# Turning the residual at five seams by DMA instead of TensorE, with two chunks by tiles of tokens, in a two-layer mixer trunk

## The chip, the cores and the metric

One core of one Trainium2 chip runs the kernel. The metric is the device time of one execution in microseconds; lower is better. Engines are called as in the profile: PE is TensorE, DVE is VectorE, ACT is ScalarE, POOL is GpSimd, SP is SyncE, which here only issues DMAs.

## What is computed

256 tokens (two tiles of 128) of width 1024 pass two layers, in float32. Each layer is

```
x = x + 1/2 * SwiGLU_1(RMSNorm(x))                    # 1024 -> 2 x 2816 -> 1024
u = RMSNorm(x);  [q|k|v|g|p|c|gates] = u @ W_in       # mixer input, blocks of 512 columns
x = x + (sig(g_ret)*y_ret + sig(g_pool)*y_pool + sig(g_conv)*y_conv) @ W_out
x = x + 1/2 * SwiGLU_2(RMSNorm(x))
```

and a last RMSNorm follows. The three branches are a chunkwise retention with rotary, a multi-scale mean pooling, and a gated causal convolution of 31 taps with a LayerNorm. Between two of these stages stands what is called a seam here: x is complete for the one, and needed turned (features on partitions) by the next. There are five seams besides the kernel's start: in layer 0 after the first FFN, before the second FFN, then between the layers, and the first two again in layer 1.

## The kernel before

**Products.** Every big product is made in three matmuls: the weights and the turned activations are each split in a high part of type fp32r and the rest (`w_hi`, `w_lo`, `xT_hi`, `xT_lo`), and `product` adds high by high, high by low and low by high in PSUM. The activations are the operand that is loaded (128x128), the weights the one that moves (512 columns). `in_block(l, g, t)` makes chunk g (1024 x 512) for tile of tokens t: 8 products of three, 24 matmuls. `wide` makes 1024 output columns from some 128-row tiles, as two halves n = 0, 1 of 512 columns. The order is written out by hand, in a function for each engine; there is no scheduler.

**Weights.** They come in halves of chunks, 1 MB each, through a ring of seven slots (`raw`, in which `w_lo` is made in place), all from SyncE's queue, in order of use. ScalarE casts a half to `w_hi` (`cast(hf)`, ring of five), VectorE makes `w_lo` (`sub(hf)`). A load waits until the half seven before it is used, a cast until the half five before it is used (`wait_half_used`); a half is used once both tiles of tokens have passed it.

**Hidden activations.** In an FFN, the product of silu and gate is turned by the DMA: ScalarE splits the four bytes of each value into two planes of 16 bits (`split_h`, tile `h_planes`), SyncE issues a DMA transpose of the planes (`turn_h`, tile `hT_planes`), VectorE joins them (`h_merge`, tile `hT_whole`). SyncE issues it in its stream of loads, behind a load with a given number.

**The seam.** VectorE adds the product to x, one quarter (tile of tokens t, 512 columns c) at a time (`add_next`). `turn_x` has TensorE transpose the quarter in four matmuls with the identity into PSUM (`tr`, two banks). ScalarE makes `xT_hi` with the norm's gain (`x_high`, 4 instructions), VectorE `xT_lo` (`x_low`, 4 instructions). The quarters of tokens 0 are turned amid the last chunk's products of tokens 1, those of tokens 1 amid the next stage's first block of tokens 0. `finish` and `begin` are the other engines' parts of this. The norm's scale comes later (`rs`), on the block's result, from `square` on ScalarE and GpSimd's `norm_factor`.

**The mixer's VectorE.** It also computes the 124 convolution taps, which are placed by hand in groups, `conv_taps(l, n)`, between other work; `decayed` scales the retention's scores into `st`, for which `inner` on TensorE waits.

**The end.** For each tile of tokens: add to x, square and sum on ScalarE, power on GpSimd, scale by ScalarE and VectorE, store.

Of the kernel before, what the change touches and what calls it, by code (L numbers as in the profile page):

```python
# [15 lines left out]
P = 128  # L16
L = 2
# [55 lines left out]
def out_bank(n):  # L73
    return 1 - n
# [23 lines left out]

ADDS_BEFORE = {0: CHUNKS - 1, 1: MIX - 1, 3: FFN2 - 1}


def trunk(nc, x_in, positions, weights_in, gate_bias, pool_scale, norm_final, params, ident_in,
          inv_freq_in, decay_in, band_in, out):
    with ExitStack() as ctx:
# [29 lines left out]
        end_small = sb("end_small", [P, 5, T])  # L134
        end_meansq = end_small[:, 0:2, :]
        end_eps, end_total, end_rs = (end_small[:, i, :] for i in range(2, 5))
# [35 lines left out]
        hT_whole = place("hT_whole", [P, 2, S])  # L172
        ffn_end, end[0] = end[0], arena_at
# [56 lines left out]
        x_hi_ready = sem("x_hi_ready")  # L230
        hT_hi_ready = sem("hT_hi_ready")
# [45 lines left out]
        end_weighted = sem("end_weighted")  # L277
        out_ready = [sem(f"out_ready{n}") for n in (0, 1)]
# [10 lines left out]
        def gain(l, norm, k):  # L289

            if l == 0 and norm == 0:
                return ident_gain[:, P + k:P + k + 1]
            return par[:, l, PAR_GAIN[norm] + k:PAR_GAIN[norm] + k + 1]

# [39 lines left out]
        def _(pe):  # L334
# [28 lines left out]
            def in_block(l, g, t, norm=None, mid={}):  # L363
# [4 lines left out]
                for k in range(KT):  # L368
# [7 lines left out]
                    if norm is not None and k % 4 == 0:  # L376
                        wait_tr_taken(pe, ("x", l, norm, t, k // 4))
# [8 lines left out]

            def wide(l, g, use, t, lhs, ks, first, last, mid={}):
# [3 lines left out]
                for n in (0, 1):  # L391
                    b = out_bank(n)
                    if first:
                        wait_acc_free(l, use, t, n, b)
                    for i, k in enumerate(ks):
                        hf = l * HALVES + 2 * g + i // m
                        if t == 0 and n == 0 and i % m == 0:
# [3 lines left out]
                                     first and i == 0, last and i == len(ks) - 1)  # L401
# [13 lines left out]
            def turn_x(l, norm, t, c):  # L415
                if l == 0 and norm == 0:
                    pe.wait_ge(x_landed[t][c], 16)
                elif norm == 0:
                    wait_acc_taken(pe, l - 1, FFN2 + FB, t, c)
                else:  # L420
                    wait_acc_taken(pe, l, FB if norm == 1 else M_OUT, t, c)
                transpose4(("x", l, norm, t, c),
# [23 lines left out]
            def ffn(l, f, after):  # L446

                g0, norm = f * FFN2, 3 * f
                in_block(l, g0, 0, norm, {3: lambda: turn_x(l, norm, 1, 0),
                                          5: lambda: turn_x(l, norm, 1, 1)} if l + f == 0 else  # L450
                         {1: lambda: turn_x(l, norm, 1, 0), 4: lambda: turn_x(l, norm, 1, 1)})
                in_block(l, g0, 1, norm)
                for b in range(1, FB):
# [1220 lines left out]
```

## Time and profile before

| | |
|---|---|
| time, median of 3 runs | 1152.99 us (1152.76 to 1153.17) |
| the profiled execution's own time | 1152.98 us |
| its span in the trace | 1151.1 us |
| TensorE busy | 1140.0 us |
| VectorE busy | 780.0 us |
| ScalarE busy | 608.7 us |
| granted clock of TensorE | 0.999 of full |
| DMA | 234.70 MB, mean 204 GB/s |

The span runs from the first to the last instruction that the profiler saw; the time has a little around it. Busy times are sums over the whole span. A matmul's record is longer than the distance to the next one, since they are pipelined: what it costs is that distance. In a group's row, the numbers behind the first bar are busy us and mean ns of one, behind the second the idle time ahead of it and what ended it.

### The profile page before, as it was taken

The numbers are of one execution on the slowest core, as the hardware profiler recorded it, in microseconds if no ns is written. First come the engines' busy times: TensorE is split into PE (matmuls) and PEld (weight loads), VectorE is DVE, ScalarE is ACT, GpSimd is POOL, SyncE is SP. The second block draws the span as 40 slices with busy tenths as digits, with TensorE's granted clock in tenths as the row PEclk, the third lists the DMA queues.
The fourth block names the chain that finished last, engine by engine and source line by source line (L and its number), as shares of the span: only waits on it lengthen the run. The fifth ranks groups of instructions, "written<-read, shape, count | busy, mean of one in ns | idle before, by whom it ended". The sixth has DMA issues, their size and how long they took to land.

```text
span 1151.1 us, 13215 instructions
## 1 busy us (share of the span) xinstructions
PE 1140.0 (99%) x5150; PEld 939.9 (82%) x5150; DVE 780.0 (68%) x953; ACT 608.7 (53%) x703; POOL 41.9 (4%) x67
## 2 busy tenths in 40 slices
PE   8999999999999999999999999999999999999997
PEld 6888888888878888888888888888888788888886
DVE  6656465699997766655465656367999976565543
ACT  7655445453655565555365554364637356555442
POOL 2000000000100010000010000020001001000000
PEclk9999999999999999999999999999999999999999
DMA  9966564563754566756576757455638645676640
GB/s 368 323 196 218 182 235 170 218 177 134 247 211 170 196 204 208 239 167 231 185 260 194 231 188 233 173 212 174 201 119 262 231 146 191 221 242 205 174 183 37
DMA packets 92942, 234.70 MB, mean 204 GB/s; under 512 B 62912, under 2 KB 63296, under 8 KB 68048
## 3 DMA queue, kind: packets, MB, share of 16 engines
q1 hardware_dynamic: 90384, 226.78, 58.6%
q0 software_dynamic: 1648, 6.06, 1.7%
q10 hardware_dynamic: 848, 1.02, 0.3%
q8 instruction: 41, 0.67, 0.2%
q14 instruction: 21, 0.17, 0.0%
HBM read 218.11 MB, written 1.05 MB: 190 GB/s over the span
## 4 chain that ended last, share of the span: by engine, by line
PE 86%; DVE 10%; ACT 2%; issue 1%; DMA 0%; POOLq 0%; ACTq 0%; DVEq 0%; POOL 0%
PE acc L352 28%; PE acc L354 28%; PE acc L353 28%; DVE y L1236 4%; DVE w_lo L1036 3%; PE tr L412 2%; ACT w_hi L675 1%; ACT pin L822 0%; DVE gates L1311 0%; DVE gates L1256 0%; DVE ua L1292 0%; DVE qk L1301 0%; DMA ident_gain<-in_ident 0%; PE tr L482 0%; DVE sideT_lo L1354 0%
## 5 line engine op out<-in xcount | busy, mean ns | idle before, releaser
L675 ACT CAST w_hi<-raw 128x2048 fp32r<-128x2048 f32 (+1 forms) x206 | 379.1, 1851 | 260.4 <-PE acc L354 255.9
L1036 DVE TENSOR_TENSOR w_lo<-raw,w_hi 128x2048 fp32r<-128x2048 f32 (+1 forms) x206 | 448.4, 2211 | 95.0 <-ACT w_hi L675 94.9
L352 PE MATMUL acc<-w_hi,xT_hi 128*128 128x512 f32 x1184 | 466.3, 394 | 1.0 <-DVE w_lo L1046 0.6
L354 PE MATMUL acc<-w_hi,xT_lo 128*128 128x512 f32 x1184 | 461.3, 390 | 0.0
L353 PE MATMUL acc<-w_lo,xT_hi 128*128 128x512 f32 x1184 | 460.9, 389 | 0.0
L352 PEld LDWEIGHTS acc<-w_hi,xT_hi 128*128 128x128 f32 x1184 | 222.4, 188 | 47.1 <-DVE gates L1311 1.5
L354 PEld LDWEIGHTS acc<-w_hi,xT_lo 128*128 128x128 f32 x1184 | 222.2, 188 | 47.0
L353 PEld LDWEIGHTS acc<-w_lo,xT_hi 128*128 128x128 f32 x1184 | 222.5, 188 | 44.4
L1099 DVE SCALAR_TENSOR_TENSOR h<-acc,rs,silu_gate 128x256 f32<-128x256 f32 x88 | 42.5, 483 | 175.2 <-ACT silu_gate L731 175.2
L352 PE MATMUL acc<-w_hi,hT_hi 128*128 128x512 f32 x352 | 137.5, 391 | 0.0
L354 PE MATMUL acc<-w_hi,hT_lo 128*128 128x512 f32 x352 | 137.0, 389 | 0.0
L353 PE MATMUL acc<-w_lo,hT_hi 128*128 128x512 f32 x352 | 136.9, 389 | 0.0
L731 ACT ACTIVATE silu_gate<-acc,rs 128x256 f32<-128x256 f32 x88 | 41.9, 476 | 121.7 <-PE acc L354 120.8
L1236 DVE SCALAR_TENSOR_TENSOR y<-uT,par,y 128x256 f32<-128x256 f32 x240 | 97.1, 476 | 0.0
L354 PEld LDWEIGHTS acc<-w_hi,hT_lo 128*128 128x128 f32 x352 | 66.1, 188 | 13.7
L353 PEld LDWEIGHTS acc<-w_lo,hT_hi 128*128 128x128 f32 x352 | 66.1, 188 | 13.5
L352 PEld LDWEIGHTS acc<-w_hi,hT_hi 128*128 128x128 f32 x352 | 66.1, 188 | 13.5
L716 ACT COPY h_planes<-h 128x512 uint16<-128x512 uint16 x88 | 50.1, 620 | 4.8 <-DMA hT_planes<-h_planes 4.8
L692 ACT ACTIVATE xT_hi<-tr,par 128x128 fp32r<-128x128 f32 x80 | 22.9, 369 | 36.6 <-PE tr L412 36.6
L1084 DVE COPY hT_whole<-hT_planes 128x1024 uint16<-128x1024 uint16 x44 | 33.3, 757 | 10.4 <-DMA hT_planes<-h_planes 10.3
L1053 DVE SCALAR_TENSOR_TENSOR x<-acc,x 128x512 f32<-128x512 f32 x24 | 16.5, 689 | 28.7 <-PE acc L354 28.7
L1072 DVE SCALAR_TENSOR_TENSOR xT_lo<-tr,par,xT_hi 128x128 fp32r<-128x128 f32 x80 | 22.5, 343 | 15.5 <-ACT xT_hi L692 15.0
(122 smaller groups left out, 568.2 us busy)
## 6 DMA issues: line engine op xcount, KB each, us to landing
raw<-in_weights SPq DMA_DIRECT2D x194, 1024.0 KB, 4.8
raw<-in_weights SPq DMA_DIRECT2D x10, 512.0 KB, 3.6
bias<-in_gate_bias POOLq DMA_DIRECT2D x6, 512.0 KB, 7.8
raw<-in_weights SPq DMA_DIRECT2D x8, 256.0 KB, 4.8
scale_row<-in_pool_scale POOLq DMA_DIRECT2D x2, 512.0 KB, 8.7
x<-in_x SPq DMA_DIRECT2D x3, 256.0 KB, 8.0
band<-in_band POOLq DMA_DIRECT2D x1, 768.0 KB, 6.2
hT_planes<-h_planes SPq DMA_TRANSPOSE x44, 3.1
```

The source lines that it names most:

```text
L352: nc.tensor.matmul(o, a_hi, b_hi, start=first, stop=False)
L353: nc.tensor.matmul(o, a_hi, b_lo, start=False, stop=False)
L354: return nc.tensor.matmul(o, a_lo, b_hi, start=False, stop=last)
L412: mm = nc.tensor.transpose(bank(name)[:, i * P:(i + 1) * P], s, ident)
L675: nc.scalar.copy(w_hi[:, hf % HIGHS, 0:n], raw[:, hf % RAWS, 0:n]).then_inc(hi_split, 1)
L692: nc.scalar.activation(xT_hi[:, k, tokens(t)], bank(("x", l, norm, t, c))[:, i * P:(i + 1) * P], ACT.Copy, scale=gain(l, norm, k)).then_in ...
L716: nc.scalar.copy(h_planes[:, :, :, t, :], h[:, t, :].bitcast(U16).rearrange("p (k n a) -> p a k n", k=2, a=2)).then_inc(h_split, 1)
L731: nc.scalar.activation(silu_gate[:, t, :], acc[:, t, IN_BANK[g], 0:256], ACT.Silu, scale=rs[:, t:t + 1]).then_inc(silu_ready, 1)
L1036: nc.vector.tensor_tensor(w_lo[:, hf % RAWS, 0:n], raw[:, hf % RAWS, 0:n], w_hi[:, hf % HIGHS, 0:n].bitcast(F32), ALU.subtract).then_inc(l ...
L1084: nc.vector.tensor_copy(hT_whole[:].rearrange("p k n -> p (k n)").bitcast(U16) .rearrange("p (m a) -> p a m", a=2), hT_planes[:]).then_inc ...
L1099: nc.vector.scalar_tensor_tensor(h[:, t, :], acc[:, t, IN_BANK[g], 256:512], rs[:, t:t + 1], silu_gate[:, t, :], ALU.mult, ALU.mult).then_ ...
L1236: a = nc.vector.scalar_tensor_tensor(y[:, c, :], u, par[:, l, w:w + 1], y[:, c, :], ALU.mult, ALU.add)
```

## The change

1. At the five seams (`SEAM`) x is turned as the hidden activations are. Each quarter is split into planes by ScalarE (`split_x`), turned by a DMA transpose from SyncE (`turn_x`), joined by VectorE (`x_join`) into `x_whole`; `x_high` and `x_low` then read that and not PSUM. The planes are those of the hidden activations, one set. TensorE transposes x only at the kernel's start.
2. TensorE's order. An FFN's last two output chunks, and the two of `W_out`, are run for tokens 0 both, and then for tokens 1 both. The next stage's first two chunks are run in the same way (`two_blocks`): both for tokens 0, then both for tokens 1.
3. The order on ScalarE and VectorE around the seams follows (`seam`), and the first blocks' silu, hidden and take steps after it.
4. Some `conv_taps` and one `sub` in the mixer are moved; the wait of the conv product is made in two steps.
5. At the end, the last chunk's product for tokens 1, columns 512 to 1023, is made in two pieces of 256 columns in a bank of its own (`last_products`), each added, squared and weighted by itself; the chunks before it are closed and added earlier.

```diff
+SEAM = {key: i for i, key in enumerate([(0, 1), (0, 3), (1, 0), (1, 1), (1, 3)])}
...
+        x_planes = h_planes[:].rearrange("p a k t n -> p a (k t) n")
+        xT_planes = hT_planes
+        x_whole = hT_whole[:].rearrange("p k n -> p (k n)").rearrange("p (k n) -> p k n", n=P)
...
                     if norm is not None and k % 4 == 0:
-                        wait_tr_taken(pe, ("x", l, norm, t, k // 4))
+                        if (l, norm) in SEAM:
+                            pe.wait_ge(x_lo_ready, piece(l, norm, t, k // 4) + 1)
+                        else:
+                            wait_tr_taken(pe, ("x", l, norm, t, k // 4))
...
+            def two_blocks(l, g, norm, mid={}):
+
+                in_block(l, g, 0, norm)
+                in_block(l, g + 1, 0)
+                in_block(l, g, 1, norm, mid)
+                in_block(l, g + 1, 1)
...
+                    closed = last or (l, g, t, n) == (L - 1, CHUNKS - 2, 1, 1)
...
+                if after:
+                    for t in range(T):
+                        step(final - 1, t)
+                        step(final, t)
+                else:
+                    for i in (final - 1, final):
+                        step(i, 0)
+                        step(i, 1)
...
+            def last_products(l, g, ks):
+
+
+                m = len(ks) // 2
+                for i, k in enumerate(ks):
+                    hf = l * HALVES + 2 * g + i // m
+                    mm = product(acc[:, 1, out_bank(0), :], hT(k, 1), weights(hf, i % m * D, NB),
+                                 False, i == len(ks) - 1)
+                done(mm, (l, g, 1, 0))
+                for part in (0, 1):
+                    for i, k in enumerate(ks):
+                        hf = l * HALVES + 2 * g + i // m
+                        mm = product(ret[:, part, 0:256], hT(k, 1),
+                                     weights(hf, i % m * D + NB + part * 256, 256),
+                                     i == 0, i == len(ks) - 1)
+                    done(mm, (l, g, 1, 1 + part))
...
-                in_block(l, M_A, 0, 1, {1: lambda: turn_x(l, 1, 1, 0),
-                                        4: lambda: turn_x(l, 1, 1, 1)})
-                in_block(l, M_A, 1, 1)
-                in_block(l, M_B, 0)
-                in_block(l, M_B, 1, mid={3: lambda: turn_u(l, 0)})
+                two_blocks(l, M_A, 1, {5: lambda: turn_u(l, 0)})
...
-                pe.wait_ge(conv_lo_ready, l * 2 + 2)
-                wide(l, M_CONV, M_CONV, 0, side, range(4), True, True)
+                pe.wait_ge(conv_lo_ready, l * 2 + 1)
+                wide(l, M_CONV, M_CONV, 0, side, range(4), True, True,
+                     {(0, 1): lambda: pe.wait_ge(conv_lo_ready, l * 2 + 2)})
...
+                wait_tr_taken(pe, ("m", l, 0, 1))
+                wide(l, M_OUT + 1, M_OUT, 0, xT, range(4, 8), False, True)
                 wait_tr_taken(pe, ("m", l, 1, 0))
                 wide(l, M_OUT, M_OUT, 1, xT, range(4), True, False)
-                wait_tr_taken(pe, ("m", l, 0, 1))
-                wide(l, M_OUT + 1, M_OUT, 0, xT, range(4, 8), False, True)
                 wait_tr_taken(pe, ("m", l, 1, 1))
-                wide(l, M_OUT + 1, M_OUT, 1, xT, range(4, 8), False, True,
-                     {(0, 0): lambda: turn_x(l, 3, 0, 0), (0, 2): lambda: turn_x(l, 3, 0, 1)})
+                wide(l, M_OUT + 1, M_OUT, 1, xT, range(4, 8), False, True)
...
+            def turn_x(l, norm, t, c):
+                at = piece(l, norm, t, c)
+                sp.wait_ge(x_split, at + 1)
+                sp.wait_ge(x_joined, at)
+                sp.dma_start_transpose(xT_planes[:].rearrange("p a (g n) -> p (a g) n", n=P),
+                                       x_planes.rearrange("p a k n -> p (a k n)")
+                                       ).then_inc(x_turned, 16)
...
+                for at, norm in ((0, 0), (MIX, 1), (FFN2, 3)):
+                    if (hf // HALVES, norm) in SEAM:
+                        for ahead, t, c in ((2, 0, 0), (2, 0, 1), (5, 1, 0), (6, 1, 1)):
+                            if hf % HALVES == 2 * at + ahead:
+                                turn_x(hf // HALVES, norm, t, c)
...
+            def split_x(l, norm, t, c):
+
+                wait_x(l, norm, t, c)
+                act.wait_ge(x_turned, 16 * piece(l, norm, t, c))
+                nc.scalar.copy(x_planes,
+                               x[:, t, columns(c)].bitcast(U16)
+                               .rearrange("p (k n a) -> p a k n", k=4, a=2)).then_inc(x_split, 1)
...
+            def seam(l, norm, hf):
+
+                split_x(l, norm, 0, 0)
+                square(l, norm, 0)
+                split_x(l, norm, 0, 1)
+                x_high(l, norm, 0, 0)
+                cast(hf + 1)
+                cast(hf + 2)
+                x_high(l, norm, 0, 1)
+                split_x(l, norm, 1, 0)
+                cast(hf + 3)
+                split_x(l, norm, 1, 1)
                 x_high(l, norm, 1, 0)
+                cast(hf + 4)
+                square(l, norm, 1)
                 x_high(l, norm, 1, 1)
...
+            def x_join(l, norm, t, c):
+
+                dve.wait_ge(x_turned, 16 * (piece(l, norm, t, c) + 1))
+                dve.wait_ge(x_lo_ready, piece(l, norm, t, c))
+                nc.vector.tensor_copy(hT_whole[:].rearrange("p k n -> p (k n)").bitcast(U16)
+                                      .rearrange("p (m a) -> p a m", a=2), xT_planes[:]
+                                      ).then_inc(x_joined, 1)
...
+            def seam(l, norm, hf):
+
                 add_next(l, norm, 0, 0)
                 add_next(l, norm, 0, 1)
+                x_join(l, norm, 0, 0)
                 x_low(l, norm, 0, 0)
+                x_join(l, norm, 0, 1)
+                sub(hf + 1)
                 add_next(l, norm, 1, 0)
                 x_low(l, norm, 0, 1)
+                add_next(l, norm, 1, 1)
+                sub(hf + 2)
+                x_join(l, norm, 1, 0)
+                sub(hf + 3)
+                x_low(l, norm, 1, 0)
+                x_join(l, norm, 1, 1)
+                sub(hf + 4)
+                x_low(l, norm, 1, 1)
...
-                conv_taps(l, 18)
+                conv_taps(l, 14)
...
-                conv_taps(l, 8)
+                conv_taps(l, 12)
...
+            add_last(acc[:, 1, out_bank(1), :], columns(1), (L - 1, CHUNKS - 2, 1, 0))
...
+            for part in (0, 1):
+                s = slice(NB + part * 256, NB + part * 256 + 256)
+                dve.wait_ge(end_added, part + 1)
+                add_last(ret[:, part, 0:256], s, (L - 1, CHUNKS - 1, 1, 1 + part))
+                dve.wait_ge(end_added, part + 2)
+                weigh(1, s)
+            dve.wait_ge(end_weighted, 5)
+            scale_out(1)
```

How this moves instructions, at the first seam (end of layer 0's first FFN, start of the mixer). In `order`'s rows a name is the tile's. **VectorE, before**, from the adds of tokens 0 (x2) to the subtractions after the seam; the rows of `w_lo` are `sub`, those of `xT_lo` are `x_low`:

```order
L1053 SCALAR_TENSOR_TENSOR x<-acc,x 128x512 x2
L1072 SCALAR_TENSOR_TENSOR xT_lo<-tr,par,xT_hi 128x128 x4
L1053 SCALAR_TENSOR_TENSOR x<-acc,x 128x512
L1072 SCALAR_TENSOR_TENSOR xT_lo<-tr,par,xT_hi 128x128 x4
L1053 SCALAR_TENSOR_TENSOR x<-acc,x 128x512
L1036 TENSOR_TENSOR w_lo<-raw,w_hi 128x2048
L1072 SCALAR_TENSOR_TENSOR xT_lo<-tr,par,xT_hi 128x128 x8
L1366 MEMSET uT 128x4x30
L1036 TENSOR_TENSOR w_lo<-raw,w_hi 128x2048 x2
```

**VectorE, now**, from the same two adds; `hT_whole<-hT_planes` is `x_join`:

```order
L1170 SCALAR_TENSOR_TENSOR x<-acc,x 128x512 x2
L1187 COPY hT_whole<-hT_planes 128x2x512
L1198 SCALAR_TENSOR_TENSOR xT_lo<-hT_whole,par,xT_hi 128x128 x4
L1187 COPY hT_whole<-hT_planes 128x2x512
L1153 TENSOR_TENSOR w_lo<-raw,w_hi 128x2048
L1170 SCALAR_TENSOR_TENSOR x<-acc,x 128x512
L1198 SCALAR_TENSOR_TENSOR xT_lo<-hT_whole,par,xT_hi 128x128 x4
L1170 SCALAR_TENSOR_TENSOR x<-acc,x 128x512
L1153 TENSOR_TENSOR w_lo<-raw,w_hi 128x2048
L1187 COPY hT_whole<-hT_planes 128x2x512
L1153 TENSOR_TENSOR w_lo<-raw,w_hi 128x2048
L1198 SCALAR_TENSOR_TENSOR xT_lo<-hT_whole,par,xT_hi 128x128 x4
```

Three of the four joins are in these rows; the fourth follows, with the `sub` of A+4 and the last `x_low`. A is the mixer's first half of weights. The three `sub` shown are those of A+1 (the first block's second half), A+2 and A+3 (the second block's second half); the last stands right behind the third join, where before the last two `x_low` (the x8) stood ahead of the `sub` of A+3 (in the x2).

**SyncE, before**, the loads between the FFN's last turns of `h` and the mixer's first turns of q and k:

```order
L636 DMA raw<-in_weights 128x2048 x2
L601 DMA_TRANSPOSE hT_planes<-h_planes 128x8x128
L636 DMA raw<-in_weights 128x2048 x19
L610 DMA_TRANSPOSE qkT_planes<-qk_planes 128x8x128 x2
L636 DMA raw<-in_weights 128x2048 x2
L610 DMA_TRANSPOSE qkT_planes<-qk_planes 128x8x128 x2
```

**SyncE, now**, from the last turn of `h`; L661 is `turn_x`:

```order
L653 DMA_TRANSPOSE hT_planes<-h_planes 128x8x128
L696 DMA raw<-in_weights 128x2048 x8
L661 DMA_TRANSPOSE hT_planes<-h_planes 128x8x128 x2
L696 DMA raw<-in_weights 128x2048 x3
L661 DMA_TRANSPOSE hT_planes<-h_planes 128x8x128
L696 DMA raw<-in_weights 128x2048
L661 DMA_TRANSPOSE hT_planes<-h_planes 128x8x128
L696 DMA raw<-in_weights 128x2048 x7
L670 DMA_TRANSPOSE qkT_planes<-qk_planes 128x8x128 x2
```

Of the four turns of x, the first two are issued behind the load of A+2, the third behind that of A+5 and the fourth behind that of A+6. The one behind A+5 is thus issued when three loads have gone out since the second turn: A+3, A+4 and A+5.

## Rows read from the trace of the kernel before

**Rows 1.** The page, busy time by engine:
```profile
PE 1140.0 (99%) x5150; PEld 939.9 (82%) x5150; DVE 780.0 (68%) x953; ACT 608.7 (53%) x703; POOL 41.9 (4%) x67
```

**Rows 2.** TensorE timeline, 100 to 104 us: start, length, operation; first and last:
```profile
99.65 0.39 PE L352 MATMUL acc<-w_hi,xT_hi 128*128 128x512 f32 x1
...
103.96 0.39 PE L353 MATMUL acc<-w_lo,xT_hi 128*128 128x512 f32 x1
```

**Rows 3.** Groups by line, TensorE:
```profile
L412 PE MATMUL tr<-ident_gain,x 128*128 128x128 f32 x96 | 14.9, 279 | 1.0 <-DMA x<-in_x 0.6 <-DMA ident_gain<-in_ident 0.4
```

**Rows 4.** Waits of TensorE: us in total, times, longest us:
```profile
PE ret L501 <- DVE st L1284: 1.3, 2, 0.6
...
PE acc L352 <- DVE sideT_lo L1354: 0.4, 2, 0.2
```

**Rows 5.** Timeline at the first seam, TensorE around a four of transposes:
```profile
185.10 0.39 PE L354 MATMUL acc<-w_hi,hT_lo 128*128 128x512 f32 x1
...
186.93 0.39 PE L354 MATMUL acc<-w_hi,hT_lo 128*128 128x512 f32 x1
```

**Rows 6.** Timeline of VectorE in the first mixer, ahead of `decayed`:
```profile
266.19 7.21 DVE L1236 SCALAR_TENSOR_TENSOR y<-uT,par,y 128x256 f32<-128x256 f32 x18
```

**Rows 7.** Timeline of TensorE in the pool product, first and ninth row:
```profile
299.96 0.28 PE L352 MATMUL acc<-w_hi,sideT_hi 128*128 128x256 f32 x1
...
300.92 0.28 PE L354 MATMUL acc<-w_hi,sideT_lo 128*128 128x256 f32 x1
```

**Rows 8.** Groups by line and shape, operations like those of the last stage:
```profile
L1099 DVE SCALAR_TENSOR_TENSOR h<-acc,rs,silu_gate 128x256 f32<-128x256 f32 x88 | 42.5, 483 | 175.2 <-ACT silu_gate L731 175.2
L1053 DVE SCALAR_TENSOR_TENSOR x<-acc,x 128x512 f32<-128x512 f32 x24 | 16.5, 689 | 28.7 <-PE acc L354 28.7
...
L1013 ACT ACTIVATE squares<-x 128x512 bf16<-128x512 f32 x4 | 2.5, 631 | 18.0 <-DVE x L1053 18.0
```

**Rows 9.** Groups by line and shape, ScalarE, then VectorE:
```profile
L675 ACT CAST w_hi<-raw 128x2048 fp32r<-128x2048 f32 x194 | 368.3, 1910 | 249.0 <-PE acc L354 244.5 <-DMA raw<-in_weights 4.5
...
L802 ACT COPY qk_planes<-qk 128x1024 uint16<-128x1024 uint16 x8 | 8.3, 1036 | 0.0
...
L1036 DVE TENSOR_TENSOR w_lo<-raw,w_hi 128x2048 fp32r<-128x2048 f32 x194 | 436.8, 2283 | 95.0 <-ACT w_hi L675 94.9
...
L1084 DVE COPY hT_whole<-hT_planes 128x1024 uint16<-128x1024 uint16 x44 | 33.3, 757 | 10.4 <-DMA hT_planes<-h_planes 10.3
...
L1072 DVE SCALAR_TENSOR_TENSOR xT_lo<-tr,par,xT_hi 128x128 fp32r<-128x128 f32 x80 | 22.5, 343 | 15.5 <-ACT xT_hi L692 15.0
```

**Rows 10.** Instructions on tile hT_planes, SyncE: the 44 turns, and their landings:
```profile
L601 SPq DMA_TRANSPOSE hT_planes<-h_planes x44: 1232/1232/1392, 29.8 to 1088.8; - x44
...
DMA to landing us min/median/max: 3.0/3.1/9.7
```

**Rows 11.** The page, DMA issues: KB each, median us from issue to landing:
```profile
raw<-in_weights SPq DMA_DIRECT2D x194, 1024.0 KB, 4.8
```

**Rows 12.** Tile raw, the second load of a pair: at 384.6, at 191.2:
```profile
DMA to landing us min/median/max: 6.6/6.6/6.6
...
DMA to landing us min/median/max: 7.8/7.8/7.8
```

**Rows 13.** Tile raw, the five loads from 5.1 to 7.4 us:
```profile
L636 SPq DMA_DIRECT2D raw<-in_weights x5: 453/473/693, 5.1 to 7.4; - x5
...
DMA to landing us min/median/max: 10.2/14.0/17.8
```

**Rows 14.** A load at 233.9, then a turn of qk_planes at 234.7:
```profile
L636 SPq DMA_DIRECT2D raw<-in_weights x1: 327/327/327, 233.9 to 233.9; - x1
...
DMA to landing us min/median/max: 5.6/5.6/5.6
...
L610 SPq DMA_TRANSPOSE qkT_planes<-qk_planes x1: 1231/1231/1231, 234.7 to 234.7; - x1
...
DMA to landing us min/median/max: 5.7/5.7/5.7
```

More of the change, by code:

```diff
@@ L770, in ffn @@
+                for b in range(2, FB):
+                    silu(l, f, b - 1, 1)
+                    cast(ahead(b))
+                    split_h(l, f, b - 1, 0)
+                    split_h(l, f, b - 1, 1)
+                    silu(l, f, b, 0)
+                    h_high(l, f, b - 2)
+                    cast(ahead(b) + 1)
+                final = len(OUT_CHUNKS) - 1
+                for i in range(final):
+                    hf = ahead(FB + i)
                     if i == 0:
@@ L988, in mixer @@
                 merged_high(l, 1, 1)
-                cast(ahead(M_OUT) + 1)
-                finish(l, 3, ahead(M_OUT + 1))
+                seam(l, 3, ahead(M_OUT))
             act.wait_ge(ident_landed, 16)
@@ L1022, in _ @@
                               weighted[:, t, columns(0)]).then_inc(stored, 16)
+            for n in (0, 1):
+                wait_acc_taken(act, L - 1, FFN2 + FB, 0, n)
+                last_square(0, columns(n), n)
+            store(0)
+            wait_acc_taken(act, L - 1, FFN2 + FB, 1, 0)
+            last_square(1, columns(0), 0)
+            for part in (0, 1):
+                act.wait_ge(end_added, part + 2)
+                last_square(1, slice(NB + part * 256, NB + part * 256 + 256), 1 + part)
+            store(1)
         @block.vector
@@ new lines, in ffn @@
+                if l + f == 0:
+                    x_low(0, 0, 1, 0)
+                    x_low(0, 0, 1, 1)
+                    for hf in (2, 3, 4):
+                        sub(hf)
+                    hidden(l, f, 0, 0)
+                    hidden(l, f, 0, 1)
+                    sub(ahead(1) - 1)
+                    sub(ahead(1))
+                    hidden(l, f, 1, 0)
+                else:
+                    hidden(l, f, 0, 0)
+                    hidden(l, f, 1, 0)
+                    sub(ahead(1) - 1)
+                    hidden(l, f, 0, 1)
+                    sub(ahead(1))
@@ L1151, in ffn @@
                         dve.wait_ge(par_landed, 16)
-                    finish(*after, l * HALVES + 2 * (g0 + FFN_CHUNKS - 1) + 3)
+                    seam(*after, ahead(FFN_CHUNKS - 2))
             setup = [0]
```

259 lines of the change are left out of this document (140 added, 119 removed).

## The prediction, made before the run

> **What bounds the kernel now.** I read the page first, then TensorE's groups, its waits, its timeline in a quiet stretch and at a seam, then the other engines' groups by shape, and last the landings of single transfers. The page is there to name the engine: TensorE is busy for 1140.0 of 1151.1 us [rows 1]. The quiet stretch gives its beat: from the first to the last row shown, 19 matmuls lie 4.31 us apart, 0.227 us each, though one lasts 0.39 us [rows 2]. So time can only come out of matmuls that need not be there, out of waits, and out of the two ends. The groups show such matmuls: 96 transposes of x in 24 fours [rows 3]. The waits show nearly nothing else: 1.3 us at the retention's inner products (twice 0.6) and 0.4 us at the conv side (twice 0.2); none is at a seam [rows 4]. Whatever replaces the transposes must therefore arrive in time, as they do now.
>
> **What goes.** The seam's timeline prices a four: the matmul before it starts at 185.10, and the sixth product matmul after that one at 186.93 [rows 5]. Six beats are 1.36 us, so the four costs 0.47 us. Five seams have four such groups each; the first four groups of the kernel stay. Twenty by 0.47 is 9.4 us off the path.
>
> The two waits named above are served by other edits. Four conv taps are moved from ahead of `decayed` to behind it; 18 taps take 7.21 us, so four take 1.6 us, more than the 0.6 us for which TensorE waits on `st` [rows 6, 4]. The conv side's wait is split so that the first half's products start on the first half. I take both away whole: 1.7 us.
>
> At the end, the last 512 columns are made as two pieces of 256. A 256-column matmul has a beat of 0.12 us (0.96 us for eight) [rows 7], so 24 of them take 2.88 us where twelve whole ones took 2.72: +0.16. Behind the last one, a DVE operation of 256 columns takes 0.48 against 0.69 us, and the square 0.63 us for 512 columns, of which I save 0.2 (between nothing and half) [rows 8]. Net about -0.3 us, and between +0.2 and -0.5. What follows (the power, the scaling, the store) is as long as before.
>
> So 9.4 + 1.7 + 0.3 = 11.4 us are to be had if nothing new is late.
>
> **What is added.** Each of the 20 pieces of x (512 columns of 128 tokens) now takes a split by ScalarE, like the row of `qk_planes`, 1.04 us; a DMA transpose of eight tiles, like the row of `hT_planes`; and a join by VectorE, 0.76 us [rows 9, 10]. Casting and subtracting are as before. This costs VectorE 20 x 0.76 = 15 us and ScalarE 21 us, off the path only as long as the next wait is met. The chain has one set of planes, so the pieces go one after another.
>
> I lay out one seam with a clock that is 0 when TensorE issues the last matmul for tokens 0, columns 0 of the stage's product, plus one beat. TensorE's new order gives the dates. Twelve matmuls are 2.72 us, a block for one tile of tokens is 5.44 us. Tokens 0 are complete at 2.72. Then tokens 1 of the last two chunks run to 13.60. The next stage's first block on tokens 0 runs from 13.60 to 19.04, its second block on tokens 0 to 24.48, and tokens 1 follow. Call the next stage's weight halves A, A+1, and so on. Halves A-4, A-3, A-2 and A-1 come free at 6.80, 8.16, 12.24 and 13.60, since tokens 1 are done last. Each end is seen some 0.2 us later (0.39 less a beat).
>
> Piece (0,0): add 0.2 to 0.9, split to 1.95, turn of 3.0 to 5.0, join to 5.75. Its split and cast for TensorE are ready near 8, wanted at 13.6. Piece (0,1): split to 6.0, turn issued at 6.05, landed at 9.05. On ScalarE the casts of A+1 and A+2 (1.9 us each [rows 9]) stand ahead of its `x_high`, and start at 7.1, when A-4 is free; so `x_high`, 1.1 us like the low part (four of 0.34 us, overlapping by a little [rows 9]), ends at 11.9 and the low part near 13.7, wanted at 16.3. Neither is late.
>
> Piece (1,0) is the one in danger. VectorE adds it at 12.0 to 12.7, ScalarE splits it to 13.7, and SyncE issues its turn at 13.75. But SyncE's order, shown with the change, puts this turn **behind the load of A+5**, which went out at 12.4. And in the queue A+5 itself stands behind A+3 (out at 7.3, when turn (0,1) has been issued) and A+4 (out at 8.4). A lone load lands after 4.8 us [rows 11]: A+3 at 12.1. The second load of a close pair, issued 1.36 us after its forerunner, lands after 6.6 us at one seam and 7.8 at another [rows 12], which is 3.2 or 4.3 us after the one ahead. In a queue that stays full, at the kernel's start, five loads issued from 5.1 to 7.4 land between 15.3 and 25.2, 2.5 us apart [rows 13]. I put A+4 between the two rows of pairs, at 15.7, and A+5 by the full queue 2.5 us behind it, at 18.2. A turn behind a load: that load went out at 233.9 and took 5.6, the turn at 234.7 and took 5.7, so it landed 0.9 us after the load [rows 14]. Turn (1,0) then lands at **19.1**, over 5 us after its issue and not 3.
>
> On VectorE `x_join` waits for this landing, and `sub(A+3)` is queued behind it, though its cast was done near 15.6. Join to 19.85, subtraction of 2.28 us [rows 9] to 22.1. TensorE wants A+3 in the middle of the second block, at 21.76, with the weight load a beat ahead: 21.54. **It waits 0.6 us.** The rest just holds: piece (1,1) is split to 20.2, its turn lands at 23.2 (A+6 ahead of it at 21.6), join to 23.9, `sub(A+4)` to 26.2, the last low part to 27.3; TensorE, itself 0.6 late, wants it at 27.6. Later halves (A+5 on) find their slots free at 27.4 and are wanted at 38, so they are not late.
>
> Bounds of this wait: if loads in the queue are no slower than lone ones, A+5 lands at 17.2 and the turn at 18.1; the subtraction ends at 21.1 and nothing waits. With the slower row of pairs, used for both loads, A+4 lands at 16.2, A+5 at 20.5, the turn at 21.4, the subtraction ends at 24.4: 2.9 us. I take 0.6 five times, +3.0 us.
>
> A rule speaks against the whole change. The rows have the turn of eight tiles at 3.0 us at the least and 3.1 in the median [rows 10]. The Trainium skill, VectorE: DVE Perf Modes, Rules for kernel authors, says to transpose 128x128 on TensorE where PSUM will do as the destination, and to go to the DMA crossbar only otherwise; The three transpose paths on that page gives 1309 ns a tile by DMA against 390 ns. By that price eight tiles are 10.5 us, an estimate from the page: with turn (1,0) issued at 13.75 it lands at 24.2, TensorE waits 5.7 us a seam, and the sum would be 1152.98 - 11.4 + 28.5 = 1170. The traces say a third of that for the DMA, and 0.47 us for four tiles on the path, so here the trace disagrees with the page's price in both columns.
>
> **The sum.** The profiled execution took 1152.98 us (span 1151.1 and 1.9 around it), the median of the runs shown is 1152.99, so the two may be used alike. 1152.98 - 9.4 - 1.7 - 0.3 + 3.0 = **1144.6 us**.
>
> **Rivals.**
> No seam wait at all: the turn lands by 18.5. For it: the median turn of 3.1 us, and a layout in which 0.6 us is all that is missing. Against: three loads are put into the queue within 5.2 us ahead of it. 1152.98 - 11.4 = 1141.6 us.
>
> The wait eats the gain: the third load behind two takes the 3.2 to 4.3 us of a pair's second and not 2.5, the turn lands near 20.8, the subtraction ends near 23.8 and each seam waits 1.8 to 2.7 us: 1150.6 to 1155.1 us. The even point is 11.4 / 5 = 2.3 us a seam. For it: 7.8 us of one close second load. Against: 6.6 us in the other row, and 2.5 us a load at the start.
>
> Slower than before: the same place, with turn (1,0) landing after 21.4, at the slow bound or beyond. Waits of 2.9 us give 1152.98 - 11.4 + 14.5 = 1156.1 us. It decides from a landing of 21.4 on. For it: what is paid at A+3 may be paid again at piece (1,1), which has 0.3 us of slack.
>
> A turn that is slow in itself: one turn took 9.7 us [rows 10]. If such were the rule among loads, (1,0) would land at 23.4, the subtraction end at 26.4, the wait be 4.9 us and the time 1152.98 - 11.4 + 24.5 = 1166 us. The page's rule above would end on this side. Against: the median is 3.1.
>
> That the edits don't do what they say is possible for the taps alone: then 1.3 us less is gained.
>
> **How the numbers follow.** A measurement of this kernel tells some 0.2%, 2.3 us, from no change. Forecast, a wait of 0.2 to 1.8 us a seam (1142.6 to 1150.6): 0.55. No wait: 0.22. Gain eaten, within 0.2% of before: 0.10. Slower by the queue: 0.10; by slow turns: 0.03. Faster is 0.55 + 0.22 = 0.77, same 0.10, slower 0.13. The range 1141 to 1152 takes in the first two and half of the third, and leaves out some 0.18; the likeliest case's own is 1142.6 to 1150.6.
>
> **What would show it.** Right: 16 transposes of x left on TensorE; a wait of TensorE at `w_lo` some 0.6 us long, five times, each in the second block of a stage; `x_join` idle on the DMA just before; landings of turns near 3 us for the first two of a seam and over 5 for the third; no wait at `st`. Wrong: no wait at `w_lo` (time near 1141.6), or waits at `xT_lo` or over 2.3 us a seam, or new waits in the mixer that this layout doesn't have.

## The result, and the profile after

The changed kernel takes 1159.19 us (median of 5 runs, 1155.65 to 1160.7) against 1152.99 us: ratio 1.0048, interval 1.0036 to 1.006. It is **slower by 0.5%**. Forecast was 1144.6 us, faster, with a range of 1141.0 to 1152.0. Sign and size are wrong.

The profiled execution took 1155.65 us, the fastest of the five. Its page, busy time by engine, answers to [rows 1]:

```profile
PE 1132.8 (98%) x5082; PEld 933.5 (81%) x5082; DVE 794.1 (69%) x976; ACT 630.2 (55%) x725; POOL 41.7 (4%) x68
```

TensorE is busy for 7.2 us less, and yet the span grew from 1151.1 to 1153.8 us. The groups by line, the first of which answers to [rows 3] (busy, mean ns, idle time ahead and what ended it):

```profile
L439 PE MATMUL tr<-ident_gain,x 128*128 128x128 f32 x16 | 2.8, 300 | 0.4 <-DMA ident_gain<-in_ident 0.4
...
L766 ACT COPY h_planes<-x 128x1024 uint16<-128x1024 uint16 x20 | 20.9, 1046 | 60.4 <-DMA hT_planes<-h_planes 29.2
...
L1187 DVE COPY hT_whole<-hT_planes 128x1024 uint16<-128x1024 uint16 x20 | 15.2, 761 | 36.0 <-DMA hT_planes<-h_planes 36.0
```

Sixteen transposes are left, and splits and joins cost what was forecast (1.04 and 0.76 us). But VectorE stood idle for 36 us in front of its 20 joins, until a turn landed. TensorE's waits, which answer to [rows 4]:

```profile
PE acc L367 <- DVE w_lo L1153: 11.3, 5, 3.6
PE acc L367 <- DVE w_lo L1163: 1.5, 2, 1.0
PE ret L630 <- DVE scale_row L1143: 1.2, 1, 1.2
...
PE acc L367 <- DVE xT_lo L1198: 0.2, 1, 0.2
```

The waits at `st` and `sideT_lo` are gone. The five at `w_lo` are there, once a seam, in the place named (L1163 is at the kernel's start); each is 2.3 us and not 0.6. VectorE's timeline at the first seam (start, length, operation, idle time ahead) shows what they wait for:

```profile
190.73 2.28 DVE L1153 TENSOR_TENSOR w_lo<-raw,w_hi 128x2048 fp32r<-128x2048 f32 x1
198.22 0.75 DVE L1187 COPY hT_whole<-hT_planes 128x1024 uint16<-128x1024 uint16 x1 [5.21 <-DMA hT_planes<-h_planes]
198.86 2.28 DVE L1153 TENSOR_TENSOR w_lo<-raw,w_hi 128x2048 fp32r<-128x2048 f32 x1
```

The join of piece (1,0) waits 5.2 us for its turn, and the subtraction of A+3 is queued behind it; TensorE starts again at 201.20, just as that ends. The turn, and the load of A+5 ahead of it (tiles hT_planes and raw, SyncE):

```profile
L661 SPq DMA_TRANSPOSE hT_planes<-h_planes x1: 2176/2176/2176, 190.3 to 190.3; - x1
...
DMA to landing us min/median/max: 7.9/7.9/7.9
...
L696 SPq DMA_DIRECT2D raw<-in_weights x1: 327/327/327, 188.7 to 188.7; - x1
...
DMA to landing us min/median/max: 8.4/8.4/8.4
```

The load lands at 197.1 and the turn at 198.2. On the seam's clock, where this seam's 0 is 176.3:

| | forecast | the five seams |
|---|---|---|
| turns (0,0), (0,1) land after | 3.0 | 3.0, 3.0 |
| A+3 lands | 12.1 | 12.5 to 12.9 |
| A+4 lands | 15.7 | 15.2 to 15.8 |
| turn (1,0) issued | 13.75 | 13.9 |
| A+5 lands | 18.2 | 20.8, 19.5, 19.1, 19.8, 20.5 |
| turn (1,0) lands | 19.1 | 21.9, 20.4, 20.2, 20.9, 22.5 |
| turn (1,1) lands | 23.2 | 24.4 to 26.8 |

A+3 landed 0.4 to 0.8 us later than forecast and A+4 only 2.5 to 3.0 behind it, where the forecast had 3.6: that A+4 comes out right is two errors that cancel.

One thing stands in no row of the forecast. At the fourth seam TensorE comes back from its wait, and soon its clock is not the full one (timeline; then the windows: busy of PE, PEld, DVE, ACT, POOL, granted clock, DMA share, GB/s):

```profile
768.61 0.50 PE L367 MATMUL acc<-w_hi,xT_hi 128*128 128x512 f32 x1 [2.00 <-DVE w_lo L1153]
...
771.06 0.63 PE L368 MATMUL acc<-w_lo,xT_hi 128*128 128x512 f32 x1
771.48 0.63 PE L369 MATMUL acc<-w_hi,xT_lo 128*128 128x512 f32 x1
```

```profile
768.00:772.00 4.00, 3.39 (x10) 2.68 (x11) 3.12 (x7) 3.48 (x6) 1.09 (x2) 0.69 0.60 70
772.00:776.00 4.00, 4.00 (x17) 3.29 (x16) 3.13 (x7) 1.81 (x4) 2.16 (x2) 0.89 0.00 0
```

The matmuls lie 0.43 us apart where 0.227 is the beat: for 3.4 us the clock is at its lower level, 1.2 GHz, and that costs 4 x 0.31 + 4 x 0.11 = 1.7 us. At the same kind of wait in the other seams of this execution it didn't fall. The other four executions have no kept trace, but their mean clock was lower and their time longer: 0.996 at 1157.26 and 1159.19 us, 0.994 at 1160.54 and 1160.7, against 0.998 here.

### The profile page after: what moved, and what is told of

Read it like the earlier page. It is cut to its first block, busy times and chain, and to the rows that moved or that the text cites. A ratio compares the mean times of both kernels' runs of the same rounds, so it can differ in the third digit from the quotient of the medians.

```text
span 1153.8 us, 13189 instructions
## 1 busy us (share of the span) xinstructions
PE 1132.8 (98%) x5082; PEld 933.5 (81%) x5082; DVE 794.1 (69%) x976; ACT 630.2 (55%) x725; POOL 41.7 (4%) x68
## 4 chain that ended last, share of the span: by engine, by line
PE 79%; DVE 9%; DMA 6%; ACT 3%; issue 2%; POOLq 0%; ACTq 0%; DVEq 0%; POOL 0%; SPq 0%
PE acc L367 26%; PE acc L369 26%; PE acc L368 26%; DMA hT_planes<-h_planes 6%; DVE w_lo L1153 4%; DVE y L1380 1%; ACT h_planes L766 1%; PE tr L439 1%; DVE hT_whole L1187 1%; ACT w_hi L741 1%; DVE x L1170 1%; ACT pin L930 0%; DVE gates L1455 0%; DVE ua L1436 0%; DVE gates L1400 0%
## 5 line engine op out<-in xcount | busy, mean ns | idle before, releaser
L367 PE MATMUL acc<-w_hi,xT_hi 128*128 128x512 f32 x1184 | 466.3, 394 | 13.2 <-DVE w_lo L1153 11.3
L797 ACT COPY h_planes<-h 128x512 uint16<-128x512 uint16 x88 | 50.4, 620 | 11.3 <-DVE h L1228 6.8
L766 ACT COPY h_planes<-x 128x1024 uint16<-128x1024 uint16 x20 | 20.9, 1046 | 60.4 <-DMA hT_planes<-h_planes 29.2
L1211 DVE COPY hT_whole<-hT_planes 128x1024 uint16<-128x1024 uint16 x44 | 33.4, 759 | 13.1 <-DMA hT_planes<-h_planes 13.1
L1187 DVE COPY hT_whole<-hT_planes 128x1024 uint16<-128x1024 uint16 x20 | 15.2, 761 | 36.0 <-DMA hT_planes<-h_planes 36.0
L1673 POOL TENSOR_TENSOR meansq_eps<-meansq,small 128x1 f32<-128x1 f32 x12 | 10.0, 832 | 651.6 <-ACT squares L789 651.6
```

The costliest lines, as they stand in the source:

```text
L367: nc.tensor.matmul(o, a_hi, b_hi, start=first, stop=False)
L766: nc.scalar.copy(x_planes, x[:, t, columns(c)].bitcast(U16) .rearrange("p (k n a) -> p a k n", k=4, a=2)).then_inc(x_split, 1)
L797: nc.scalar.copy(h_planes[:, :, :, t, :], h[:, t, :].bitcast(U16).rearrange("p (k n a) -> p a k n", k=2, a=2)).then_inc(h_split, 1)
L1187: nc.vector.tensor_copy(hT_whole[:].rearrange("p k n -> p (k n)").bitcast(U16) .rearrange("p (m a) -> p a m", a=2), xT_planes[:]).then_inc ...
L1211: nc.vector.tensor_copy(hT_whole[:].rearrange("p k n -> p (k n)").bitcast(U16) .rearrange("p (m a) -> p a m", a=2), hT_planes[:]).then_inc ...
```

## The experiments

All but e4 are edits of the changed kernel. **e1: both turns of tokens 1 one load earlier.** (An entry of the list names the load behind which a turn is issued, then the piece.)

```diff
-for ahead, t, c in ((2, 0, 0), (2, 0, 1), (5, 1, 0), (6, 1, 1)):
+for ahead, t, c in ((2, 0, 0), (2, 0, 1), (4, 1, 0), (5, 1, 1)):
```

> SyncE issues the third turn of x of a seam ahead of the load of A+5 instead of behind it, and the fourth ahead of A+6; nothing else is changed against the changed kernel. Theory Q (the wait is made by the place in SyncE's queue): the third turn goes out at 13.9 on the seam's clock, A+4 lands at 15.5, the turn 1 us behind it near 16.5 to 17, and the subtraction of A+3 ends near 20; no wait of TensorE at w_lo or xT_lo; all of 11.4 us is kept: 1141.6 us, between 1140.8 and 1143, and the granted clock stays at 0.999 because TensorE no longer stops. Rival R (turns and loads slow each other in whatever order they are issued): the third turn still lands 6 us or more after its issue, waits of some 2 us a seam stay, time 1150 or more. Rival C (the clock's falls have nothing to do with the waits): waits go but the clock stays at 0.994 to 0.998 and the time near 1145 to 1149.

Measured: **1141.68 us** (1141.44 to 1142.1), ratio 0.9902 (0.9889 to 0.9916). TensorE's waits, and the turn of piece (1,0) at the first seam:

```profile
PE ret L630 <- DVE scale_row L1143: 1.2, 1, 1.2
PE acc L367 <- DVE w_lo L1163: 1.0, 2, 0.6
PE tr L439 <- DMA ident_gain<-in_ident: 0.6, 1, 0.6
PE acc L367 <- DVE xT_lo L1198: 0.3, 1, 0.3
```

```profile
L661 SPq DMA_TRANSPOSE hT_planes<-h_planes x1: 1238/1238/1238, 190.7 to 190.7; - x1
...
DMA to landing us min/median/max: 3.0/3.0/3.0
```

No wait is left at `w_lo` of a seam. The turn is issued at the same 13.9 and lands at 17.0 (17.6 once) instead of 20.2 to 22.5. Two turns moved ahead of one load each are worth 17.5 us, and turn a loss of 0.5% into a gain of 1.0%.

**e2: take the subtraction out from behind the join.**

```diff
 sub(hf + 2)
-x_join(l, norm, 1, 0)
 sub(hf + 3)
+x_join(l, norm, 1, 0)
 x_low(l, norm, 1, 0)
```

> The changed kernel with the subtraction of A+3 ahead of the third join on VectorE. Theory Q with the block at VectorE: the waits at w_lo (11.3 us in five) go, but the turn lands as late as now (20 to 22 on the seam's clock, 24 in the last), so the third piece's low part ends 3.3 us behind that and is wanted at 24.3: TensorE waits at xT_lo 0 to 1.2 us in four seams and some 3 us in the last, in sum 3 to 6 us, time 1145 to 1149. If VectorE's queue were not the block, the waits at w_lo would stay and the time be that of the changed kernel, 1155 to 1160.

Measured: 1155.99 us (1155.13 to 1158.17), ratio 1.0028 (1.0017 to 1.0039); less gain than any theory had. The wait moves from the weights to x (the list; then the first seam, which has two of the nine waits):

```profile
PE acc L367 <- DVE xT_lo L1198: 10.6, 9, 2.4
...
201.11 0.47 PE L367 MATMUL acc<-w_hi,xT_hi 128*128 128x512 f32 x1 [0.28 <-DVE xT_lo L1198]
...
206.43 0.50 PE L367 MATMUL acc<-w_hi,xT_hi 128*128 128x512 f32 x1 [2.35 <-DVE xT_lo L1198]
```

With A+3 in time, TensorE stops later. For piece (1,0) that is little, 0.3 to 0.5 us at four seams. The most of it, 0.9 to 2.4 us at every seam and 9.0 us in sum, is for piece (1,1), which the expectation left out: its turn lands at 26.2 at the first seam, and behind its join another subtraction stands ahead of its low part. In all it is 10.6 us against 11.3, and the profiled execution lost 3.4 us more to two falls of the clock, each behind a wait of 2.3 us. The queue on VectorE chose where the wait showed, and the landing of the turns set most of its size.

**e3: the turn one load later.**

```diff
-for ahead, t, c in ((2, 0, 0), (2, 0, 1), (5, 1, 0), (6, 1, 1)):
+for ahead, t, c in ((2, 0, 0), (2, 0, 1), (6, 1, 0), (6, 1, 1)):
```

> The dose the other way: the third turn goes out behind the loads of A+5 and A+6, nothing else changed. Theory Q: it lands 3 to 4 us later than now, each seam's wait grows from 2.3 to 5 or 6 us, in sum 26 to 30 us, time 1168 to 1180 with more falls of the clock. Rival R: the order does not matter, the time stays within 2 us of the changed kernel.

Measured: 1176.42 us (1173.86 to 1178.37), ratio 1.0202 (1.0185 to 1.0218). Load A+6 goes out at 13.8, just ahead of the turn at 14.2, and lands at 22.0 to 23.0; the turn lands at 23.0 to 24.8. The waits, and the windows around the end of the first seam's wait, at 204.1:

```profile
PE acc L367 <- DVE w_lo L1153: 25.0, 5, 5.8
```

```profile
200.00:203.00 3.00, 0.00 (x0) 0.00 (x0) 1.83 (x2) 1.78 (x4) 0.00 (x0) 0.88 0.10 20
203.00:206.00 3.00, 1.87 (x4) 1.50 (x5) 2.42 (x6) 3.00 (x4) 0.00 (x0) 0.50 0.53 90
206.00:210.00 4.00, 4.00 (x13) 3.17 (x12) 3.96 (x9) 3.06 (x10) 3.20 (x3) 0.61 0.00 0
210.00:214.00 4.00, 4.00 (x21) 3.34 (x20) 1.36 (x4) 1.87 (x2) 0.00 (x0) 1.00 0.20 43
```

The waits doubled (5 us a seam), and now the clock falls at each of them: in TensorE's records it is at the lower level for 6.8 us four times and for 3.4 us once, 30.6 us in all, of which half is lost, 15.3 us. Here it fell at about 202.3, 1.8 us before the wait ended, and of those nothing is lost: half of 0.9 to 2.5 us less, four times, 3.3 us. So 13.2 us more of waits (27.8 in all against 14.6), 15.3 - 1.7 more of the clock, less 3.3: 23.5 us over the changed kernel's span. Measured: 1176.6 - 1153.8 = 22.8.

**e4: the small parts alone, put into the kernel before** (the taps, the split wait, the end in two pieces, and one subtraction in the mixer that the change moves too).

```diff
-                conv_taps(l, 18)
+                conv_taps(l, 14)
...
-                pe.wait_ge(conv_lo_ready, l * 2 + 2)
-                wide(l, M_CONV, M_CONV, 0, side, range(4), True, True)
+                pe.wait_ge(conv_lo_ready, l * 2 + 1)
+                wide(l, M_CONV, M_CONV, 0, side, range(4), True, True,
+                     {(0, 1): lambda: pe.wait_ge(conv_lo_ready, l * 2 + 2)})
```

> The kernel before with only the small edits: four conv taps behind decayed, the sub in the mixer moved, the conv product's wait in two steps, and the end in two pieces. Theory as predicted: 1.7 us of waits and 0.3 us at the end, 1151.0 us. Rival: the waits for st and sideT_lo only hide another wait behind them, and the end costs as much as it saves: 1152.5 to 1153.2 us.

Measured: 1150.12 us (1149.76 to 1150.22), ratio 0.9975 (0.9965 to 0.9984): 2.9 us, where the sum had 1.7 + 0.3. Its list of waits has neither `st` nor `sideT_lo`. The excess has a place in the trace of before:

```profile
272.98 0.39 PE L354 MATMUL acc<-w_hi,xT_lo 128*128 128x512 f32 x1
273.99 0.38 PE L501 MATMUL ret<-v,st 128*128 128x128 f32 x1 [0.62 <-DVE st L1284]
```

The list counts 0.62 us from the end of one matmul to the start of the next. But matmuls overlap: start to start it is 1.01 us, and to the next start 0.21 more, where e4's trace has 0.23 and 0.11 at this place. So that wait cost 0.88 us, twice, and the conv side's in the same way (0.59 and 0.34 for 0.23 and 0.23) 0.47 us, twice: 2.7 us for the 1.7 of the list. The end (last matmul to the span's end) went from 6.2 to 5.8 us; but traces with the same new end have 5.8 to 6.4, so what it gained isn't shown.

**e5: the turns of tokens 1 in ScalarE's queue**, issued there right behind the split, so that no load of SyncE's stands ahead of them.

```diff
-for ahead, t, c in ((2, 0, 0), (2, 0, 1), (5, 1, 0), (6, 1, 1)):
+for ahead, t, c in ((2, 0, 0), (2, 0, 1)):
...
+                if t == 1:
+                    ...
+                    act.dma_start_transpose(xT_planes[:].rearrange("p a (g n) -> p (a g) n", n=P),
```

> The changed kernel with the two turns of tokens 1 issued from ScalarE's own DMA queue right after their splits; the loads stay where they are in SyncE's queue. Theory Q in its strict form (a turn is late because it stands behind A+5 in the same queue): in a queue of its own it lands 3 to 5 us after its issue, near 17 to 19 on the seam's clock, no wait of TensorE at w_lo, 1141 to 1144 us. Rival S (the 16 DMA engines are full of the three loads, and a turn needs all of them, whichever queue it is in): it lands 5 to 8 us after its issue, waits of 0.5 to 2 us a seam stay, 1146 to 1156 us.

Measured: 1176.96 us (1172.8 to 1177.63), ratio 1.0196 (1.0174 to 1.0218); 24.3 us of waits at `w_lo`, longest 6.1. The turn at the first seam:

```profile
L773 ACTq DMA_TRANSPOSE hT_planes<-h_planes x1: 2330/2330/2330, 190.7 to 190.7; - x1
...
DMA to landing us min/median/max: 11.0/11.0/11.0
```

With the turns out of SyncE's list, load A+6 goes out at 190.47, 0.2 us ahead of the turn, and lands at 199.46; the turn, though alone in its queue, lands at 201.71. "It waits because it stands behind a load in the same queue" falls. e3 is the control: there too A+6 goes out just ahead of the turn, by some 0.4 us, but the turn is in SyncE's queue, and the result is the same (1176.42 us; landing 8.8 to 10.5 us after issue, against 9.4 to 11.0 here).

What holds in every trace here is that a turn lands behind all loads in flight when it is issued, whichever queue they are in: of the 796 turns of the eleven traces (of x, h, q and k, and the retention), 618 are issued with a load in flight, and none lands ahead of one. The kernel before shows it across queues already. Its slowest turn of `h`, 9.7 us [rows 10], is issued from SyncE at 29.83, lands at 39.5, and has ahead of it a load that GpSimd issued at 29.27 and that lands at 38.9 (turn; then load):

```profile
L601 SPq DMA_TRANSPOSE hT_planes<-h_planes x1: 1392/1392/1392, 29.8 to 29.8; - x1
...
DMA to landing us min/median/max: 9.7/9.7/9.7
...
L1536 POOL DMA_DIRECT2D scale_row<-in_pool_scale x1: 540/540/540, 29.3 to 29.3; - x1
...
DMA to landing us min/median/max: 9.6/9.6/9.6
```

**e6: fill TensorE's wait**: nine unused matmuls (2.0 us) at the place of each seam's wait. They write a PSUM bank that nothing else uses at that time.

```diff
+            def fill(l, g, n):
+                for _ in range(n):
+                    nc.tensor.matmul(ret[:, 0, :], xT_hi[:, 0, tokens(0)],
+                                     weights(l * HALVES + 2 * g, 0, NB)[0], start=True, stop=True)
...
-                in_block(l, g + 1, 0)
+                in_block(l, g + 1, 0, mid={3: lambda: fill(l, g, 9)})
```

> The changed kernel with nine matmuls of 512 columns more (2.0 us) in each seam's second block, at the place where TensorE waits for the subtraction of A+3, their result unused. They need nothing that is late, so they only fill the wait. Theory C (a long stop of TensorE makes the granted clock fall for 3.4 us, and these falls are what the changed kernel costs beyond its waits and scatters by): the waits at w_lo shrink from 11.3 us to 2 to 4 us in sum, the clock stays near 0.999, the time is 1153 to 1155 us and scatters by less than 1.5 us. Rival: the falls come whatever TensorE does there; the time is 1158 to 1162 us at 0.994 to 0.996.

Measured: 1156.18 us (1154.64 to 1157.94, ten runs), ratio 1.0026 (1.0017 to 1.0036). The profile has no fall of the clock, and of the seams' waits (L1158 here)

```profile
PE acc L367 <- DVE w_lo L1158: 1.7, 3, 0.8
```

TensorE does 10.2 us of useless work (45 x 0.227), the waits at the seams shrink from 11.5 to 1.9 us, and the kernel is 3.0 us faster than without it (medians; the means differ by 2.5, with a standard error of 1.0). As work and waits sum up to about the same, the gain is what the fallen clock costs: the mean clock is 0.998 to 1.000 in these ten executions and was 0.994 to 0.998 in the five of the changed kernel. Ten executions still lie 3.3 us apart (five of the changed kernel: 5.1), though I had put the scatter down to the clock. That the landings vary from run to run would explain it, but only one execution has a trace, so this is not shown.

**e7: e1, but the FFN's last two chunks chunk by chunk again**, at three of the five seams (all but those behind the mixer).

```diff
-                if after:
-                    for t in range(T):
-                        step(final - 1, t)
-                        step(final, t)
-                else:
-                    for i in (final - 1, final):
-                        step(i, 0)
-                        step(i, 1)
+                for i in (final - 1, final):
+                    step(i, 0)
+                    step(i, 1)
```

> The kernel of the first experiment (turns ahead of the loads) with one part of the change undone: the FFN's last two output chunks run chunk by chunk again instead of tokens by tokens (three of the five seams; those after W_out keep the new order). Tokens 0 are then complete 5.4 us later against the next stage's start. By the layout the first piece's low part is ready 8 us after its product and is wanted at 7.9, the second's near 12 and wanted at 10.7: TensorE waits 1 to 3 us at each of the three seams, in sum 3 to 9 us, with the clock falling now and then; 1145 to 1153 us. Rival: the DMA turn alone brings the gain and the order is not needed: within 1 us of 1141.7.

Measured: 1156.8 us (1155.98 to 1157.43), ratio 1.0032 (1.002 to 1.0044). 15 us more than e1: `xT_lo` 9.9 us in 8 waits, longest 2.4. Of the 14.4 us between the two spans (1154.7 and 1140.3), 10.4 are waits (13.5 against 3.1), 1.7 are one fall of the clock, and the rest is about what nine more stops cost beyond the gaps that the list counts. The order by tokens' tiles is what gives the chain of add, split, turn and join its time.

**e8: both turns of tokens 1 ahead of the load of A+5; e9: the same, and in the first mixer the gates' input ahead of the sines.**

```diff
-for ahead, t, c in ((2, 0, 0), (2, 0, 1), (4, 1, 0), (5, 1, 1)):
+for ahead, t, c in ((2, 0, 0), (2, 0, 1), (4, 1, 0), (4, 1, 1)):
```

```diff
+                gated_u(l, 0)
...
-                gated_u(l, 0)
```

> The turning kernel with the list of SP's issues changed so that both turns of tokens 1 stand ahead of load A+5 (in the run with one turn ahead it was (4,1,0), (5,1,1); now (4,1,0), (4,1,1)). Theory (a turn is as long as the loads in flight make it, and lands behind those issued before it): turn (1,1) is issued near 18.1 on the seam's clock as before and lands 3.0 us later, near 21.2, where it had landed 21.3 to 23.5; load A+5 goes out near 19.3, almost alone, and lands near 24, 3.4 us ahead of its cast at 27.4. The last waits of TensorE at a seam (xT_lo 0.3 us) go; time 1141.0 to 1141.8, against 1141.68 of the run with one turn ahead. Rival (the raw buffers are now late: A+5 and A+6 land behind their casts): TensorE waits at w_lo with 1 us or more at a seam, time 1146 or more.

> The kernel with both turns ahead, and in the first mixer gated_u(l,0) written before the sines on ScalarE and VectorE, so that the two gaps of TensorE behind gated_u and turn_u near 203.7 and 205.6 (0.69 and 0.53 us, against 0.24 of a start-to-start beat) have their input sooner. Theory: both gaps close, 0.5 to 0.7 us less than the kernel with both turns ahead, near 1141.0. Rival (the sines are then late for the stage that reads them, or the gaps are those of another input): the same time within 0.3 us, with the waits moved to the sine tiles or left where they are.

Measured: e8 **1140.62 us** (1140.38 to 1140.83), ratio 0.9892 (0.9877 to 0.9907); e9 **1140.36 us** (1140.09 to 1140.75), ratio 0.9891 (0.9874 to 0.9907). The turns of tokens 1 in e8's first seam, both of them:

```profile
L661 SPq DMA_TRANSPOSE hT_planes<-h_planes x2: 1232/1264/1297, 190.5 to 194.7; - x2
...
DMA to landing us min/median/max: 3.0/3.0/3.1
```

And VectorE there, where the joins no longer stand idle for long:

```profile
193.53 0.76 DVE L1187 COPY hT_whole<-hT_planes 128x1024 uint16<-128x1024 uint16 x1 [0.32 <-DMA hT_planes<-h_planes]
194.19 2.27 DVE L1153 TENSOR_TENSOR w_lo<-raw,w_hi 128x2048 fp32r<-128x2048 f32 x1
196.38 1.13 DVE L1198 SCALAR_TENSOR_TENSOR xT_lo<-hT_whole,par,xT_hi 128x128 fp32r<-128x128 f32 x4
197.74 0.76 DVE L1187 COPY hT_whole<-hT_planes 128x1024 uint16<-128x1024 uint16 x1 [0.23 <-DMA hT_planes<-h_planes]
```

Turn (1,1) now lands at 21.1 to 21.7 at all seams (21.3 to 23.6 in e1), the wait at `xT_lo` is gone, and A+5 lands at 24.6 to 25.2, before its cast at 27.4. The gain over e1, about 1 us, is smaller than the intervals of either ratio, but each of e8's four executions is shorter than each of e1's. e9's reason falls: the two gaps near 204 and 206, seen in e1's trace, are absent from e8's trace already, and 0.26 us can't be told from nothing.

## Why the prediction was wrong

**What goes** was undersized by a microsecond. e8, with no wait at a seam, is the clean measure: its span is 12.2 us below that of before (1138.9 and 1151.1), where the forecast had 11.4 to be had. The small parts gave 2.9 us and not 2.0 (e4). The other 9.4 us (1148.3 to 1138.9) are what the twenty fours were priced at, 0.47 us each. That e1 came out at the forecast's "no wait" time (1141.68 for 1141.6) is partly luck: it had a microsecond more to gain, and lost about as much to late turns of piece (1,1).

**The other times at the seam** were right (the issue of the turn, 13.9 for 13.75, the first two turns, splits and joins, and the place, kind and number of the waits), but for A+3 and A+4, whose errors cancelled.

**The step that failed** is one term: A+5 "by the full queue 2.5 us behind" A+4, at 18.2. It landed at 19.1 to 20.8, 3.9 to 5.3 us behind A+4. The 2.5 us were read from the kernel's start, where five loads are in the queue at once [rows 13]; here three loads go out in 5 us, the last of them 4.1 us behind the second. The rows of pairs [rows 12] were the nearer ones for this load: 3.2 to 4.3 us behind the one ahead. In e3 and e5, where A+6 and not the turn follows at once, A+5 landed 3.5 to 4.3 us behind A+4, just as they say; whether the turn itself made the rest isn't separated. I left those rows to a rival with 0.10. The turn came 1.0 to 2.0 us behind the load (0.9 in [rows 14]), as a mean at 21.2 and not at 19.1; 0.6 + 2.1 us is a wait of 2.7 us, measured 1.2 to 3.6, 2.3 in the mean.

That is the rival "the wait eats the gain" (landing near 20.8, waits of 1.8 to 2.7 us), and its chance was too small. By the forecast's own prices five waits of 2.3 us give 1152.9, no change. The time above that, 1155.65 in the profiled execution and 1159.19 in the median, has causes that no rival named. That it falls near the price of "slower than before", 1156.1, is luck: that rival wanted waits of 2.9 us.

**The step that was missing** is what a wait costs beyond its gap. First, a stop costs more than the list counts:

```profile
197.81 0.39 PE L369 MATMUL acc<-w_hi,xT_lo 128*128 128x512 f32 x1
201.20 0.50 PE L367 MATMUL acc<-w_hi,xT_hi 128*128 128x512 f32 x1 [3.00 <-DVE w_lo L1153]
201.53 0.39 PE L368 MATMUL acc<-w_lo,xT_hi 128*128 128x512 f32 x1
```

These two steps take 3.72 us where two beats are 0.45: 3.27 us for a gap of 3.00, and so at each of the six stops at the seams, 0.27 us more, 1.6 in sum. Second, the clock: 1.7 us in the profiled execution, about 3 in the median by e6. With both, e8's span accounts for the changed kernel's: 1138.9, plus 11.4 us more of waits (14.6 against 3.2), plus 1.6, plus 1.7, is 1153.6; measured 1153.8.

**The rule against the change**, the Trainium skill, VectorE: DVE Perf Modes, Rules for kernel authors, ended on the right side (slower) for a reason that is not the one here: an undisturbed DMA turn takes 3.0 us for eight tiles, and e8, with the five seams' turns by DMA, is 1.1% faster than before (0.8% faster than e4, which has the small parts alone). The rival of "a turn that is slow in itself" misread its row: that turn of 9.7 us was issued with seven loads in flight, six of them GpSimd's (e5).

**Still open**: why a turn lands behind loads of another queue. It was not tried with loads of another size, so whether it is the DMA engines that serve in order of issue, or the turn itself that waits for them, is not settled. The run-to-run scatter at full clock was not explained either, nor why one wait is followed by a fall of the clock and a longer one is not.

## What to carry to other kernels

A small DMA on the critical path costs what the big ones issued just before it cost: look at what the queue holds when it is issued, on every engine's queue, and put it ahead of loads that aren't wanted for another 10 us. Take the landing time of a load from rows with the same spacing of issues, not from the densest stretch. And add to a forecast stall of TensorE what its clock may lose behind it; measure a stall by starts of matmuls, not by the gap that the list of waits shows. Before calling a row an outlier, look at what was in flight at its time.

## What the runs showed that I had not expected

- The same turn takes 3.0 us (3.7 once a run) with at most the end of one load ahead (e1, e8), 6.3 to 8.6 with A+4 and A+5 in flight (the changed kernel), and 8.8 to 11.0 when A+6 is too, in SyncE's queue (e3) or in one of its own (e5).
- TensorE's granted clock fell to its lower level for 3.4 us behind one of five waits of 1.2 to 3.6 us in the changed kernel, and it was not the longest: behind the one of 2.0 us, and not those of 3.0 and 3.6. In e2 it fell behind both waits of 2.3 us, in e7 behind one of three such. It fell for 6.8 us at four of five waits near 5 us and for 3.4 at the fifth (e3, and the same in e5), and not at all behind waits under 1 us (e1, e2, e6, e7).
- Useless matmuls in the place of a wait made the kernel 3.0 us faster in the median.
